# The key latents projected first, and products of ones ahead of them, in a hybrid encoder layer

## What is computed

```python
xn = rms_norm(x, norm1_g)
proj = xn @ w_in                     # 1024 x 1472
gq, gk, gv, gg, gaf, gab, fu, cq, ckv, kr = split(proj)
o_gla  = gla_mixer(...)              # gated linear attention, chunks of 64, both directions
o_fnet = fnet_mixer(fu, fnet_w)      # 2-D Fourier transform, then mixing
o_mla  = mla_mixer(cq, ckv, kr, ...) # latents -> norm -> up-projection -> attention, 8 heads
x = x + concat(o_gla, o_fnet, o_mla) @ w_out
x = x + hier_moe(rms_norm(x, norm2_g), ...)   # 32 experts, 2 for each token
return rms_norm(x, final_norm_g)
```

## Time and profile before

| | before |
|---|---|
| median of 3 runs | 517.47 us (517.38 to 518.5) |
| profiled execution: time / span | 518.39 / 516.6 us |
| busy: TensorE, VectorE, ScalarE, GpSimd | 94%, 45%, 27%, 15% |
| chain that ended last | TensorE 64%, VectorE 13%, DMA 13%, SP's queue 7% |
| DMA in the first two slices of 12.9 us | 296 and 364 GB/s |

### The profile page before, as it was taken

How to read it: one execution, slowest core, us unless ns; L and a number is a source line. 1 busy time by engine, 2 the same in 40 slices (tenths; PEclk the granted TensorE clock), 3 DMA queues, 4 the chain that set the end, 5 groups by cost and what they waited for, 6 DMA issues and landing times.

```text
span 516.6 us, 7659 instructions
## 1 busy us (share of the span) xinstructions
PE 486.3 (94%) x2888; PEld 261.5 (51%) x2888; DVE 233.1 (45%) x579; ACT 139.4 (27%) x363; POOL 75.8 (15%) x101
## 2 busy tenths in 40 slices
PE   4999999899999999999989899999999998989894
PEld 4474444457655554455456455555555553444431
DVE  3499312977757641126763222222222222232166
ACT  4425102355667650222131011111111111112023
POOL 1000000370100000001121222222222222111000
PEclk9999999999999999999999899999999999989998
DMA  8996000010497006931499999999999999999974
GB/s 296 364 271 235 1 1 0 17 37 3 140 419 296 1 1 268 423 122 42 141 320 313 397 390 416 423 417 417 421 417 421 417 417 423 420 419 417 402 288 162
DMA packets 35542, 139.42 MB, mean 270 GB/s; under 512 B 9864, under 2 KB 11976, under 8 KB 23472
## 3 DMA queue, kind: packets, MB, share of 16 engines
q1 hardware_dynamic: 30160, 130.85, 64.8%
q0 software_dynamic: 4816, 7.85, 4.1%
q10 hardware_dynamic: 528, 0.22, 0.2%
HBM read 129.94 MB, written 16.39 MB: 283 GB/s over the span
## 4 chain that ended last, share of the span: by engine, by line
PE 64%; DVE 13%; DMA 13%; SPq 7%; issue 2%; ACT 1%; DVEq 0%; POOLq 0%; ACTq 0%
PE bank L1114 17%; PE bank L976 9%; PE bank L1127 8%; PE bank L815 7%; DMA EW<-in_moe_w_up 5%; PE bank L949 4%; DMA EW<-in_w_in 4%; SPq L644 4%; PE bank L1021 3%; PE bank L1010 3%; PE bank L1086 2%; DMA EW<-y_scratch 2%; SPq L649 2%; PE bank L893 1%; DMA y_scratch<-G,sidx 1%
## 5 line engine op out<-in xcount | busy, mean ns | idle before, releaser
L1114 PE MATMUL bank<-EW,WO 128*64 128x256 f32 x640 | 78.5, 397 | 5.1 <-DMA EW<-in_moe_w_up 2.5
L1114 PEld LDWEIGHTS bank<-EW,WO 128*64 128x64 f32 x640 | 45.0, 137 | 33.2 <-DMA EW<-in_moe_w_up 4.4
L1902 DVE TENSOR_TENSOR G<-G,bank 128x128 f32<-128x128 f32 x32 | 9.2, 288 | 107.2 <-ACT G L1482 105.0
L1482 ACT ACTIVATE G<-bank 128x128 f32<-128x128 f32 x32 | 8.9, 278 | 178.8 <-PE bank L1114 164.6
L976 PE MATMUL bank<-WO,XT 128*128 128x512 f32 x128 | 56.9, 596 | 0.0
L2127 POOL DMA_INDIRECT y_scratch<-G,sidx x30 | 30.8, 1026 | 153.8 <-DVE G L1915 138.4
L1915 DVE COPY G<-bank 128x512 f32<-128x512 f32 x32 | 22.1, 692 | 46.2 <-PE bank L1127 46.2
L1127 PE MATMUL bank<-EW,G 128*64 128x512 f32 x160 | 38.3, 599 | 0.0
L976 PEld LDWEIGHTS bank<-WO,XT 128*128 128x128 f32 x128 | 23.6, 190 | 26.9 <-issue 26.9
L949 PE MATMUL bank<-EW 96*128 96x512 f32 x64 | 32.8, 596 | 0.9 <-ACT WO L1401 0.6
L1767 DVE TENSOR_REDUCE nm<-bank 128x1 f32<-128x512 f32 x32 | 22.0, 689 | 14.3 <-PE bank L949 14.1
(11 more groups left out here) (314 smaller groups left out, 724.7 us busy)
## 6 DMA issues: line engine op xcount, KB each, us to landing
EW<-in_moe_w_down SPq DMA_DIRECT2D x20, 1024.0 KB
EW<-in_moe_w_gate SPq DMA_DIRECT2D x19, 1024.0 KB
EW<-in_moe_w_up SPq DMA_DIRECT2D x19, 1024.0 KB
y_scratch<-MIX SPq DMA_DIRECT2D x8, 512.0 KB, 8.2
WO<-in_w_out SPq DMA_DIRECT2D x2, 2048.0 KB, 12.4
MIX<-in_moe_w_gate SPq DMA_DIRECT2D x4, 1024.0 KB
MIX<-in_moe_w_up SPq DMA_DIRECT2D x4, 1024.0 KB
G<-in_moe_w_down SPq DMA_DIRECT2D x4, 1024.0 KB
```

What stands on the lines that cost most here:

```text
L1114: mm = pe.matmul(bank[BLOCK * m:BLOCK * (m + 1), 0:2 * P].rearrange("p (w n) -> p w n", w=2), xeT[:, c, par * BLOCK:(par + 1) * BLOCK], wv ...
```

## The change

- The last 160 columns of `w_in` are loaded by a DMA of their own, behind tile 0 of x and ahead of tiles 1 to 3; the part `GA:W_IN` becomes `GA:CKV`.
- x is transposed tile by tile, each tile into two banks (four chunks each). VectorE copies the first four chunks of a tile in one instruction, ScalarE the last four in four.
- The latents of the keys are projected as the tiles come: tile 0, [1, 2] 1, [3] 2, 3; then `pT1` and the rest as before, without `ckr` between `pT0` and `z`.
- TensorE begins with 18 products of `ones` into bank 7, and 8 more behind the transposes of tile 0.
- ScalarE waits for `vg` in front of the Silu, not in front of `ckvT`'s copy.
- VectorE: `add_P6(0)` between the gates of the two directions; `folded` behind the copies of `V`.
- GpSimd: scaling of `wr` and the keys' rotation as soon as their data are there; then `att`'s memset, behind P1 of unit 1; then `fw`'s, behind `vg`. `rtmp` gets a place of its own behind `w_in`.

The diff, cut to its core:

```diff
+WARM, WARM_GAP = 18, 8
 # psum_plan
-    for c in range(C):
-        ring(("xT", c))
+    for t in range(T):
+        for q in range(2):
+            ring(("xT", t, q))
+    for t in range(T):
+        ring(("ckr", t))
     ring(("pT", 1))
     ring("R")
     ring(("pT", 2))
     ring(("pT", 0))
-    for t in range(T):
-        ring(("ckr", t))
 # SP
             for t in range(T):
                 sp.dma_start(X[:, t, :], x_v[:, t, :]).then_inc(x_landed[t], 16)
+                if t == 0:
+                    sp.dma_start(w_in_sb[:, :, CKV:W_IN], w_in_v[:, :, CKV:W_IN]).then_inc(win_landed[3], 16)
             sp.dma_start(w_in_sb[:, :, GQ:GV], w_in_v[:, :, GQ:GV]).then_inc(win_landed[1], 16)
-            sp.dma_start(w_in_sb[:, :, GA:W_IN], w_in_v[:, :, GA:W_IN]).then_inc(win_landed[0], 16)
+            sp.dma_start(w_in_sb[:, :, GA:CKV], w_in_v[:, :, GA:CKV]).then_inc(win_landed[0], 16)
 # TensorE
+            pe.wait_ge(ones_ready, 1)
+            def warm(n):
+                for _ in range(n):
+                    pe.matmul(banks[7][:, 0:P], ones, ones, start=True, stop=True)
+            warm(WARM)
             pe.wait_ge(ident_landed, 16)
-            for t in range(T):
+            def transpose_x(t):
                 pe.wait_ge(x_landed[t], 16)
-                for c in range(C):
-                    ...
+                for q in range(2):
+                    ps = open_bank(("xT", t, q))
+                    for j in range(4):
+                        mm = pe.transpose(ps[:, j * P:(j + 1) * P], X[:, t, 4 * q + j:D:C], ident[:, :])
+                    close_bank(mm, ("xT", t, q))
+            def key_latent(t):
+                for q in range(2):
+                    drained(pe, ("xT", t, q))
+                by_token(("ckr", t), t, CKV, 160)
+            transpose_x(0)
+            warm(WARM_GAP)
+            pe.wait_ge(win_landed[3], 16)
+            key_latent(0)
+            transpose_x(1)
+            transpose_x(2)
+            key_latent(1)
+            transpose_x(3)
+            key_latent(2)
+            key_latent(3)
             pe.wait_ge(win_landed[1], 16)
+            by_feature(("pT", 1), GQ, 128)
 ...
-            for t in range(T):
-                by_token(("ckr", t), t, CKV, 160)
             pe.wait_ge(gate_w_landed, 16 * 8)
 # ScalarE
+            def copy_x(t):
+                ps = filled(act, ("xT", t, 1))
+                for j in range(4):
+                    ins = act.activation(xnT[:, 4 + j, t * P:(t + 1) * P], ps[:, j * P:(j + 1) * P], ACT.Copy,
+                                         scale=gain1[:, 4 + j:5 + j])
+                free_bank(ins, ("xT", t, 1))
             square_x(0)
+            act.wait_ge(first_landed, 48)
+            copy_x(0)
             square_x(1)
             square_x(2)
+            copy_x(1)
+            copy_x(2)
             square_x(3)
+            copy_x(3)
 ...
-            for t in range(T):
-                drained(act, ("vg", t))
             ps = filled(act, "ckvT")
 ...
+                    for j in range(T):
+                        drained(act, ("vg", j))
                     act.activation(sgt, vg[:, :, 256:512], ACT.Silu).then_inc(silu_gate, 1)
 # VectorE
+            def copy_x(t):
+                ps = filled(dve, ("xT", t, 0))
+                free_bank(dve.tensor_tensor(xnT[:, 0:4, t * P:(t + 1) * P], ps[:, :].rearrange("p (c n) -> p c n", c=4),
+                                            gain1[:, 0:4].unsqueeze(2).to_broadcast([P, 4, P]), ALU.mult), ("xT", t, 0))
             dve.wait_ge(first_landed, 48)
+            copy_x(0)
 ...
+            for t in range(1, T):
+                copy_x(t)
 ...
                     dve.tensor_copy(tot[:, dd], ends).then_inc(decay_sum, 1)
+                    add_P6(0)
 ...
-            add_P6(0)
 ...
-            for odd in range(2):
-                dve.tensor_tensor(folded[:, odd], ...)      # in front of the states
+            for odd in range(2):
+                dve.tensor_tensor(folded[:, odd], ...)      # behind the copies of V
 # GpSimd
-            for t in range(T):
-                drained(pool, ("vg", t))
-            pool.memset(fw, 0.0).then_inc(fnetw_zero, 1)
-            pool.memset(att.rearrange("p t h n -> p (t h n)"), 0.0).then_inc(att_zero, 1)
 ...                                                         # wr scaled, keys rotated
+            drained(pool, ("P1", 1))
+            pool.memset(att.rearrange("p t h n -> p (t h n)"), 0.0).then_inc(att_zero, 1)
+            for t in range(T):
+                drained(pool, ("vg", t))
+            pool.memset(fw, 0.0).then_inc(fnetw_zero, 1)
```

## The result

The change makes the kernel slower, by a little less than half of what was forecast (+5.2): 520.28 us (median of 8 runs, 519.32 to 520.98) against 517.8 for the kernel before (8 runs), a ratio of 1.0046 [1.0036, 1.0056], +2.4 us. The time lies inside the stated range of 517.0 to 525.8. The same two kernels taken once more on another chip gave 520.18 against 517.13, 1.0059 [1.0037, 1.0081], +3.05. The profiled execution of the kernel after has a span of 518.3 and a time of 520.1.

The account below looks back on a forecast made before the run. It took TensorE as the bound, with VectorE equally gapless up to the fourth Strassen product. Order +6.4, clock +1.2 and later moves -2.4 made +5.2 on 517.5, so 522.7 us, range 517.0 to 525.8.

Parts of the forecast that it names:

- The mechanism: Main forecast, chance 0.60: VectorE's chain bound from `R` on, TensorE stops at the fourth product, clock falls; 520.6 to 525.
- Step 1, T: At the start: `pT1` begins at T = 23.2 instead of 12.59, bounds 20.5 to 24.3, after 36 `ones` instructions and the latents.
- Step 2: At the Strassen products: VectorE's order behind `R` delays `gaT` and stops TensorE 3.6 before the fourth product; +6.4, bounds +3.7 to +7.5.
- z's wait: Before z on TensorE: z now stands right behind `pT0` and waits 1.0 for `gaT`.
- Step 3, the clock: Behind the stop at the fourth product: the granted clock falls to the lower level; +1.2, from 0 to 1.7.
- Step 4: Behind the products: moves of GpSimd, ScalarE and VectorE remove waits of 0.37, 1.68 and 0.27; -2.4, from 1.7 to 3.2.
- reaches the end one to one: From before 130 us to the end: any shift passes wholly through the expert stage, which TensorE releases step by step.
- The ports' collision: Rival, 0.08: around 33 to 37, GpSimd's `wr` scaling and key rotation hold up VectorE's sums; up to 3.0 more, 525.7.
- No fall and an earlier T: Rival, 0.12: as forecast, but the clock does not fall and `pT1` starts earlier; 518.8 to 520.6.
- Faster: Rival, 0.12: VectorE does not become the bound at the products, only TensorE's own queue counts; 513.6 to 516.3.
- The sum: Whole kernel: 6.4 + 1.2 - 2.4 = +5.2 on the median of 517.5, giving 522.7.

Follow-up runs that it names:

- sums_first: The kernel after with VectorE's four sums of weights ahead of the copy of `R`; 514.83 us, ratio 0.9940 against before.
- early_only: The kernel after with the moves behind the products undone, keeping the new start and the earlier `add_P6(0)`; 523.95 us, ratio 1.0120 against before.
- delay_x4: The kernel before with 108 products of `ones` on TensorE ahead of the first scores; median +23.3 us, ratio 1.0460.
- folded_act: The kernel before with only `folded` and ScalarE's wait for `vg` moved; 517.13 us, ratio 0.9989.
- stops_short: The kernel before with five groups of 40 products of `ones` ahead of the scores, and between them four stops of 7 ScalarE copies; 570.52 us.
- stops_idle: The kernel before with five groups of 40 products of `ones` ahead of the scores, and between them four stops of 15 ScalarE copies; 585.22 us.
- late_only: The kernel before with only the moves behind the products (ScalarE's wait, `folded`, GpSimd's order); 515.9 us, ratio 0.9949.
- no_ones: The kernel after without any product of `ones`; 521.56 us, ratio 1.0096 against before.
- after_same: The kernel after, unchanged, taken a second time on another chip; 520.18 us, ratio 1.0059 against before.

## Why the prediction was right and wrong

- **The mechanism** held up to the scores: VectorE bound from `R` on, the stop of 3.35 (3.6 forecast) at the fourth product with `add_P6(0)` as its releaser, the lower clock behind it. sums_first and early_only show it.
- **Step 1, T** was mis-sized: 22.14 (22.66 in the second trace) for 23.2. I took 130 ns for an instruction at the higher clock from "eight in 1.04". But the length of a merged row reaches to the end of its last instruction; the distance of starts in the same group, 88.66 to 89.10 for four, is 110 ns. The products in the gap run at that pace, 8.32 to 10.10 for 16 instructions, and so do the transposes, 0.88 for eight. The first 36 instructions came out nearly right (7.44 for 7.8).
- **Step 2** was right to 0.2: from `pT1`'s start to P67's are 33.82 in after, 34.0 in the forecast, with z's wait 0.86 for 1.0 and P6's 0.51 for 0.7. What T lost, the shift lost: +5.2 instead of +6.4 in the first pair of traces, +5.9 in the second.
- **Step 3, the clock**: 1.70, the upper bound that I gave, for 1.2. No part of the low stretch lay in the stop: the granted clock is 1.00 up to 56.6, 0.6 behind the product's start, and 0.50 from 56.9 to 59.9.
- **Step 4**: -3.09 for -2.4, within its bounds. I added the waits that TensorE's rows name, 0.37 + 1.68 + 0.27. From start to start more went: 0.44 at the copies ahead of `kT` (1.41 in the earlier trace rows, 0.97 in after), 1.84 from V's start to `krT`'s (5.37, now 3.53), 0.71 at the first queries (2.53, now 1.82). A wait is counted from the end of the row before it, and that end is modelled. Before's rows for the last two, with 102.39 of the earlier trace rows:

```profile
97.02 3.70 PE L858 MATMUL bank<-EW 128*128 128x512 f32 x8
...
102.85 1.03 PE L883 MATMUL bank<-EW 128*128 128x256 f32 x4
...
105.38 1.17 PE L873 MATMUL bank<-G 32*128 32x128 f32 x32
```

  I also put all of VectorE's four scalings at 0.41; they take 0.35 at best.
- **The last step failed most: "reaches the end one to one".** +3.8 and +4.5 at the scores became +2.4 and +3.05 in the medians. In the pair of traces the expert stage gave back 2.2 (227.99 to 225.76) and 0.7 (226.57 to 225.89), and with these the spans agree: 3.8 - 2.2 = 1.6 for 518.3 - 516.6 = 1.7, and 4.5 - 0.7 = 3.8 for 519.0 - 515.0 = 4.0. It is not a share of the shift (delay_x4). Nor is it shown to be a fixed gift to a late start: of the 1.4 that the two pairs lack, some 0.5 stand between before and the earlier kernels too, and the rest is within what single traces and medians differ by. I looked for it in the clock: the stop of 1.89 at the experts' start made it fall in both of before's traces (at 293.8 and 293.2) and in folded_act's, three of the nine that come there early, and in none of the eight that come later; the group behind it is then 1.7 longer. (The expectation of stops_short overlooked folded_act's.) But the stage of these three takes 227.1 on average, and that of the other six early ones, without this fall, 226.7, so the fall explains little. It is not a rule of the start either, since stops_idle, 70 us later, fell there as well. In the stage TensorE is busy 95% of the time and DMA's share is 1.01; which of them sets its length, and why before's is the longer one, is open.
- **The rivals.** The ports' collision was real and hidden in after, as the argument against it said; in late_only, where VectorE does not wait, it cost the 1.0. "No fall and an earlier T", whose time is the measured one, has it by chance: T was earlier, but the fall did come, and what brought the time down lies behind the scores. "Faster" needed VectorE not to be bound, which sums_first brings about: 514.83, inside its 513.6 to 516.3.
- **The sum:** -1.2 (T and step 2), +0.5 (clock), -0.7 (moves), together 3.8 at the scores for 5.2, and 1.4 less in the medians than at the scores. The first of these, the pace, could have been read from the rows shown; the last could not.

The Trainium skill, "TensorE: Matmul & The Clock Gate", Part 4, says that transposes do not count as activity for the clock. no_ones adds nothing to what the earlier trace rows show against it (22 transposes at 211 ns with nothing before them, and then the higher pace): ahead of its 16 fast transposes at 13.22 stand not only eight slow ones but a group of latents too, which are ordinary products.

## What to carry to other kernels

When work is moved ahead in one engine's queue, go through the other engines' lists for what stands behind the first thing that is now late: four sums that did not need `R` stood behind its copy, and that was worth 5.5 us, more than the whole change. Read the pace of an instruction from starts, not from the length of a merged row, and the worth of a wait from start to start. Engines that share a way to memory should be given their work where the other one waits anyway.

## What the runs showed of the hardware

- TensorE's instructions of 128x128 in float32 came every 110 ns at the higher level, transposes and products of `ones` alike; transposes at the lower pace every 211 ns.
- Behind each of the stops of 3.35 in after, after_same, early_only and no_ones, and of 3.76 in stops_idle, the granted clock fell, at 1.5 to 3.1 us each; the four of 1.78 in stops_short and the 1.68 of before left it where it was, and the 1.89 at the experts' start did both (it fell in 4 of 20 traces).
- GpSimd and VectorE cost each other time in both directions: a sum of two SBUF tensors 1.95 for 1.22 and 2.94 for 2.28 on VectorE, the scaling of `wr` 1.70 and 1.94 for 1.03 and the first rotation step 2.36 for 0.37 on GpSimd (the rows of 1.94 and 2.36, in after, and of 0.37, in before, stand below). A memset of GpSimd held a VectorE instruction with one SBUF input up from 0.35 to 1.82. The Trainium skill, "SBUF — State Buffer", "two separate sides", has VectorE's two-input instructions compete only with a GpSimd one that reads, which the first fit; the last, against a memset, needs its case of VectorE's faster modes, which no run here separates.

```profile
32.63 1.94 POOL L2119 TENSOR_TENSOR wr<-wr,gain 128x512 f32<-128x512 f32 x1 [15.43 <-DMA rbias<-in_moe_b_re]
34.54 2.36 POOL L2111 TENSOR_TENSOR EW<-EW,ropet 128x64 f32<-128x64 f32 x1
```

```profile
92.91 0.37 POOL L2085 TENSOR_TENSOR EW<-EW,ropet 128x64 f32<-128x64 f32 x1
```
